# Placement of the weight ring and the activations in SBUF, in a float32r hybrid decoder block on one core

## Chip, cores, metric

One Trainium2 chip, one core. The time is the device time of one execution in microseconds (us), as a median over runs. Lower is better.

## What is computed

One decoder layer for 512 tokens of width 1024, in float32. The reference, cut to what matters:

```python
def hybrid_layer(x, ...):
    h = rms_norm(x, norm_mix_pre)
    u, v_sgu, q, k, v_att, gate_a, gate_b = split(h @ w_in)          # 1024 x 6656
    a = chunked_spatial_gating(gelu(u), gelu(v_sgu), ...)            # 128-token chunks, 8 groups
    att = sliding_window_sink_attention(rotary(q), rotary(k), v_att, sinks)
    merged = sigmoid(gate_a) * (a @ w_a) + sigmoid(gate_b) * (att @ w_b)
    x = x + rms_norm(merged @ w_o, norm_mix_post)
    hf = rms_norm(x, norm_ff_pre)
    ff = square(relu(hf @ w_ff_in)) @ w_ff_out                       # 1024 x 4096 x 1024
    return x + rms_norm(ff, norm_ff_post)
```

## The kernel before

Every large product is made of three float32r products. A weight and an activation are each split into a rounded part (hi) and the rest (lo), and TensorE adds hi x hi, hi x lo and lo x hi into the same PSUM bank. That is the helper `product`, whose three matmuls are lines 1125, 1126 and 1127:

```python
def product(o, a, b, first, last):
    (a_hi, a_lo), (b_hi, b_lo) = a, b
    nc.tensor.matmul(o, a_hi, b_hi, start=first, stop=False)
    nc.tensor.matmul(o, a_hi, b_lo, start=False, stop=False)
    return nc.tensor.matmul(o, a_lo, b_hi, start=False, stop=last)
```

The first operand `a` is stationary (loaded by an LDWEIGHTS of 128x128), the second, `b`, is moving (512 columns, in one place 256). In the rows of the trace the moving operand is named first: `acc<-actB_hi,w_hi` streams actB and holds w, `acc<-w_hi,ff_hi` streams w and holds ff.

Weights come through a ring of four slots (`SLOTS`) of one unit each, 128 x 1024 values. SyncE loads a unit into `w_raw` by DMA, ScalarE rounds it into `w_hi` (`round_unit`, line 563), VectorE writes the rest into `w_lo` (`lo_of`, line 799), and TensorE waits on `lo_made` before a unit. A slot is rounded again when TensorE is done with it (`pe_done`) and loaded again when `lo_made` has passed. 132 units go through the ring.

A unit is used in one of two ways. `columns_unit` holds the weights and streams the activations (8 products of 512 columns). `rows_step` holds the activations and streams the weights (2 products for each of 4 token tiles). Both are 24 matmuls a unit.

The stages in order, all written out by hand in the block `@block.tensor`, with the activations that they use and the count of matmuls of `product`:

- q, k, v projections: 12 units by rows, actB stationary, 288 matmuls
- gates and u (called side): 24 units by columns, actB moving, 576; the 16 steps of attention lie between them (`scores`, lines 1237 and 1238: kT moving, actA stationary; `turn_probs`, line 1247; `values`, lines 1263 and 1266: pT moving, v_pair stationary)
- v of the spatial gating: 8 units by rows, actB stationary, 192
- w_b: 8 units by columns, actA moving, 192, with the 64 matmuls of the spatial mixing (line 1312) between
- w_a: 8 units by columns, actB moving, 192
- w_o: 8 units by rows, actA stationary, 192
- feed-forward, in two halves of 2048: ff-in, 16 units by columns, actB moving (384 matmuls of 512 columns; in the first half the first four units are done as two halves of 256 columns, so 192 of 256 and 288 of 512), then ff-out, 16 units by rows, ff stationary, 384

SBUF addresses are given out in the order of the calls of `keep` and `group`, upward from 16.1 KiB. Tensors that live at different times share a place: a `with ExitStack()` gives the addresses back at its end, and `region_a` and `region_b` then claim the whole stretch. Each of w_raw, w_hi, w_lo, actB_hi, actB_lo, actA_hi and actA_lo takes 16 KiB of each partition.

```python
w_raw = keep("w_raw", [P, SLOTS, UNIT])
w_hi = keep("w_hi", [P, SLOTS, UNIT], F32R)
w_lo = keep("w_lo", [P, SLOTS, UNIT], F32R)
actB_hi = keep("actB_hi", [P, KT, S], F32R)
actB_lo = keep("actB_lo", [P, KT, S], F32R)
```

Of the kernel before, what the change touches and what calls it, by code (L numbers as in the profile page):

```python
# [35 lines left out]
F32 = mybir.dt.float32  # L36
F32R = mybir.dt.float32r
# [4 lines left out]
P = 128  # L42
D = 1024
S = 512
TT = S // P
KT = D // P
# [13 lines left out]
SLOTS = 4  # L60
UNIT = KT * P
# [156 lines left out]
def hybrid_block(nc, x, positions, w_in, ln_v_gain, ln_v_bias, w_spatial, b_spatial, sinks, w_a, w_b,  # L218
# [11 lines left out]
    with ExitStack() as ctx:  # L230
# [3 lines left out]
        def keep(name, shape, dt=F32):  # L234
            return ctx.enter_context(nc.sbuf_tensor(name, shape, dt))


        w_raw = keep("w_raw", [P, SLOTS, UNIT])
        w_hi = keep("w_hi", [P, SLOTS, UNIT], F32R)
        w_lo = keep("w_lo", [P, SLOTS, UNIT], F32R)  # L240


        actB_hi = keep("actB_hi", [P, KT, S], F32R)
        actB_lo = keep("actB_lo", [P, KT, S], F32R)
        ident = keep("ident", [P, P])
        mask = keep("mask", [P, 2 * P])
        pos_i = keep("pos_i", [P, TT], I32)
# [23 lines left out]
        denom2 = keep("denom2", [P, QPK])  # L271
        r_denom = keep("r_denom", [P, QPK])

        def group(stack, spec):
            return [stack.enter_context(nc.sbuf_tensor(n, s, d)) for n, s, d in spec]

        with ExitStack() as a:
            actA_hi, actA_lo = group(a, [("actA_hi", [P, KT, S], F32R), ("actA_lo", [P, KT, S], F32R)])  # L280
        with ExitStack() as a:
            ff_sum, g_ff_post, relu_b, sq_b, junk_ff = group(a, [
                ("ff_sum", [P, TT, D], F32), ("g_ff_post", [P, D], F32), ("relu_b", [P, 2, S], F32),
                ("sq_b", [P, 2, S], F32), ("junk_ff", [P, D], F32)])
        ctx.enter_context(nc.sbuf_tensor("region_a", [P, 2 * KT * S], F32))
        with ExitStack() as a:
            kT_hi, kT_lo, v_pair, o_part, o_sum, scores_sb, gates, probs, pT_hi, pT_lo, u_sb = group(a, [
                ("kT_hi", [P, NKV, S], F32R), ("kT_lo", [P, NKV, S], F32R),
                ("v_pair", [P, TT, NKV, 2 * HD], F32R), ("o_part", [P, 2, 2, P], F32),
                ("o_sum", [P, 2, 2, P], F32), ("scores_sb", [P, QPK, 2 * P], F32),  # L290
                ("gates", [P, 2 * KT, S], F32), ("probs", [P, QPK, 2 * P], F32),
                ("pT_hi", [P, 2, QPK * P], F32R), ("pT_lo", [P, 2, QPK * P], F32R),
                ("u_sb", [P, KT, S], F32)])
# [1117 lines left out]
```

## Time and profile before

| | us |
|---|---|
| median of 2 runs | 804.77 (804.72 to 804.82) |
| span of the profiled execution, first to last instruction | 802.8 |
| around that span, against the median | 2.0 |
| TensorE matmul busy | 790.7 (98%) |
| TensorE weight load busy | 659.3 (82%) |
| VectorE busy | 415.2 (52%) |
| ScalarE busy | 322.1 (40%) |
| GpSimd busy | 60.3 (8%) |

The page of the profile gives no time of the profiled execution beside its span; the 2.0 us are the median less the span. Matmuls are pipelined, so the busy time of one (some 390 ns for 512 columns) is longer than the distance from its start to the next one's. That distance is the length of a stretch divided by the matmuls that start in it.

### The profile page before, as it was taken

Reading aid. Unit: us, or ns where it says so; the run is one execution under the profiler, and the core shown is the slowest. Engines: PE = TensorE matmul, PEld = TensorE weight load, DVE = VectorE, ACT = ScalarE, POOL = GpSimd, SP = SyncE. Lnnn points to the kernel's source line nnn. Section 1 sums busy time; section 2 is a strip of 40 time slices with the busy share of each in tenths; the row PEclk is TensorE's granted clock in tenths of the full one; section 3 lists DMA queues with packets and bytes.
Section 4 is the critical chain, followed back from the end, with each engine's and each line's share of the span. In section 5 each row is a group of like instructions: output and inputs, shape, how many; then the busy total and the mean of one; then the engine's idle time right before and its main releaser. Section 6 shows DMA issues by size and latency. Waiting matters only on the chain.

```text
span 802.8 us, 10375 instructions
## 1 busy us (share of the span) xinstructions
PE 790.7 (98%) x3736; PEld 659.3 (82%) x3736; DVE 415.2 (52%) x730; ACT 322.1 (40%) x561; POOL 60.3 (8%) x110
## 2 busy tenths in 40 slices
PE   7999999999999999999999999999999999999996
PEld 6888888888887888888888988888888888888885
DVE  5624667777775329765536655432323354432334
ACT  4523656656666651323344444322212344322211
POOL 3000000122322003000002300000000000000001
PEclk9999999999999999999999999999999999999999
DMA  8332222222122532344331243332323333323202
GB/s 288 130 107 82 76 79 78 80 75 83 54 80 83 183 102 63 112 152 172 89 97 48 84 135 124 105 101 84 105 82 103 96 87 105 103 83 103 78 1 105
DMA packets 96215, 80.22 MB, mean 100 GB/s; under 512 B 3121, under 2 KB 77873, under 8 KB 96177
## 3 DMA queue, kind: packets, MB, share of 16 engines
q1 hardware_dynamic: 95504, 79.70, 32.0%
q8 instruction: 24, 0.39, 0.2%
q10 hardware_dynamic: 672, 0.01, 0.0%
q14 instruction: 15, 0.11, 0.0%
HBM read 77.60 MB, written 2.10 MB: 99 GB/s over the span
## 4 chain that ended last, share of the span: by engine, by line
PE 96%; DVE 2%; DMA 1%; ACT 1%; issue 0%; SPq 0%; DVEq 0%; POOLq 0%; POOL 0%; ACTq 0%
PE acc L1125 30%; PE acc L1127 30%; PE acc L1126 30%; PE aux L1312 1%; PE aux L1238 1%; DMA g_pre<-in_norm_mix_pre 1%; PE aux L1247 1%; PE aux L1237 1%; PE acc L1263 1%; PE acc L1266 1%; PE aux L1220 1%; PE aux L1167 1%; DVE x L818 0%; DVE actB_lo L809 0%; ACT probs L672 0%; DVE scores_sb L938 0%
## 5 line engine op out<-in xcount | busy, mean ns | idle before, releaser
L799 DVE TENSOR_TENSOR w_lo<-w_raw,w_hi 128x1024 fp32r<-128x1024 f32 x132 | 161.3, 1224 | 201.2 <-ACT w_hi L563 200.1
L563 ACT ACTIVATE w_hi<-w_raw 128x1024 fp32r<-128x1024 f32 x132 | 138.8, 1054 | 194.0 <-PE acc L1127 191.8
L1125 PE MATMUL acc<-actB_hi,w_hi 128*128 128x512 f32 (+1 forms) x544 | 207.1, 381 | 0.0
L1127 PE MATMUL acc<-actB_hi,w_lo 128*128 128x512 f32 (+1 forms) x544 | 205.3, 377 | 0.0
L1126 PE MATMUL acc<-actB_lo,w_hi 128*128 128x512 f32 (+1 forms) x544 | 204.9, 377 | 0.0
L1127 PEld LDWEIGHTS acc<-actB_hi,w_lo 128*128 128x128 f32 x544 | 102.4, 188 | 19.0
L1126 PEld LDWEIGHTS acc<-actB_lo,w_hi 128*128 128x128 f32 x544 | 102.5, 188 | 18.1
L1125 PEld LDWEIGHTS acc<-actB_hi,w_hi 128*128 128x128 f32 x544 | 102.4, 188 | 18.0
L1125 PE MATMUL acc<-w_hi,ff_hi 128*128 128x512 f32 x256 | 101.0, 395 | 0.0
L1127 PE MATMUL acc<-w_hi,ff_lo 128*128 128x512 f32 x256 | 101.0, 395 | 0.0
L1126 PE MATMUL acc<-w_lo,ff_hi 128*128 128x512 f32 x256 | 101.0, 395 | 0.0
L1125 PE MATMUL acc<-w_hi,actB_hi 128*128 128x512 f32 x160 | 62.7, 392 | 1.3 <-DVE actB_lo L809 1.2
L1073 DVE TENSOR_TENSOR sq_b<-relu_b 128x512 f32<-128x512 f32 x32 | 22.1, 692 | 80.2 <-ACT relu_b L761 79.9
L1126 PE MATMUL acc<-w_lo,actB_hi 128*128 128x512 f32 x160 | 62.3, 389 | 0.0
L1127 PE MATMUL acc<-w_hi,actB_lo 128*128 128x512 f32 x160 | 62.3, 389 | 0.0
L761 ACT ACTIVATE relu_b<-acc 128x512 f32<-128x512 f32 x32 | 19.2, 599 | 102.1 <-PE acc L1127 102.1
L1127 PEld LDWEIGHTS acc<-w_hi,ff_lo 128*128 128x128 f32 x256 | 48.2, 188 | 11.3
L1125 PEld LDWEIGHTS acc<-w_hi,ff_hi 128*128 128x128 f32 x256 | 48.2, 188 | 11.2
L1126 PEld LDWEIGHTS acc<-w_lo,ff_hi 128*128 128x128 f32 x256 | 48.2, 188 | 11.2
L672 ACT ACTIVATE probs<-scores_sb,neg_m 128x256 f32<-128x256 f32 (+1 forms) x64 | 30.1, 471 | 31.1 <-DVE sink_m L948 31.1
L1125 PEld LDWEIGHTS acc<-w_hi,actB_hi 128*128 128x128 f32 x160 | 30.0, 188 | 7.9 <-DVE actB_lo L809 1.8
L1127 PEld LDWEIGHTS acc<-w_hi,actB_lo 128*128 128x128 f32 x160 | 30.0, 188 | 6.2
(163 smaller groups left out, 897.7 us busy)
## 6 DMA issues: line engine op xcount, KB each, us to landing
w_raw<-in_w_in SPq DMA_DIRECT2D x44, 512.0 KB, 3.9
w_raw<-in_w_ff_in SPq DMA_DIRECT2D x32, 512.0 KB, 4.0
w_raw<-in_w_ff_out SPq DMA_DIRECT2D x32, 512.0 KB, 3.7
w_raw<-in_w_b SPq DMA_DIRECT2D x8, 512.0 KB, 3.6
w_raw<-in_w_a SPq DMA_DIRECT2D x8, 512.0 KB, 3.6
w_raw<-in_w_o SPq DMA_DIRECT2D x8, 512.0 KB, 3.8
x<-in_x SPq DMA_DIRECT2D x4, 512.0 KB, 7.4
x<-in_x SPq DMA_DIRECT2D x1, 2048.0 KB, 8.5
```

What stands on the lines that cost most here:

```text
L563: nc.scalar.activation(w_hi[:, j], w_raw[:, j], ACT.Copy).then_inc(hi_made, 1)
L672: nc.scalar.activation(probs[:, h, off:], scores_sb[:, h, off:], ACT.Exp, bias=neg_m[:, h:h + 1], accum_out=denom[:, h:h + 1])
L761: nc.scalar.activation(relu_b[:, j % 2], acc[:, j], ACT.Relu).then_inc(acc_to_act, 1)
L799: nc.vector.tensor_tensor(w_lo[:, j], w_raw[:, j], w_hi[:, j].bitcast(F32), ALU.subtract).then_inc(lo_made, 1)
L1073: nc.vector.tensor_tensor(sq_b[:, j % 2], relu_b[:, j % 2], relu_b[:, j % 2], ALU.mult).then_inc(sq_made, 1)
L1125: nc.tensor.matmul(o, a_hi, b_hi, start=first, stop=False)
L1126: nc.tensor.matmul(o, a_hi, b_lo, start=False, stop=False)
L1127: return nc.tensor.matmul(o, a_lo, b_hi, start=False, stop=last)
L1167: m = nc.tensor.transpose(aux[:, 2 * (t % 2) + k // 4, (k % 4) * P:(k % 4 + 1) * P], tile[:, t, k * P:(k + 1) * P], ident[:])
L1220: m = nc.tensor.transpose(aux[:, k % 4, t * P:(t + 1) * P], qk[:, t, 2 * k:2 * k + 2].rearrange("p h d -> p (h d)"), ident[:])
L1237: nc.tensor.matmul(o, q, kT_hi[keys], start=True, stop=False)
L1238: m = nc.tensor.matmul(o, q, kT_lo[keys], start=False, stop=True)
```

## The change

Only the addresses change. No instruction is added, removed, resized or moved in the order of any engine: each engine has as many instructions as before, in the same order, with the same waits. Every line of the body moves up by one number.

Places in SBUF, in KiB from the start of the partition:

| tensors | before | after |
|---|---|---|
| w_raw | 16.1 to 32.1 | 48.1 to 64.1 |
| w_hi, w_lo | 32.1 to 64.1 | 99.5 to 131.5 |
| actB_hi, actB_lo | 64.1 to 96.1 | 16.1 to 48.1 |
| region_a: actA_hi, actA_lo; later ff_sum, g_ff_post, relu_b, sq_b, junk_ff | 99.5 to 131.5 | 64.1 to 96.1 |
| constants and small tensors (ident, mask, ssq, ...) | 96.1 to 99.5 | the same |
| kT_hi, kT_lo (131.5 to 147.5), v_pair (147.5), o_sum, scores_sb, gates, probs, pT_hi, pT_lo (199.5 to 207.5), u_sb; v_sgu, w_mix; x1, ff_hi, ff_lo (147.5 to 211.5), mix | 131.5 and up | the same |

```diff
-        w_raw = keep("w_raw", [P, SLOTS, UNIT])
-        w_hi = keep("w_hi", [P, SLOTS, UNIT], F32R)
-        w_lo = keep("w_lo", [P, SLOTS, UNIT], F32R)
 
         actB_hi = keep("actB_hi", [P, KT, S], F32R)
         actB_lo = keep("actB_lo", [P, KT, S], F32R)
+        w_raw = keep("w_raw", [P, SLOTS, UNIT])
+
+        def group(stack, spec):
+            return [stack.enter_context(nc.sbuf_tensor(n, s, d)) for n, s, d in spec]
+
+        with ExitStack() as a:
+            actA_hi, actA_lo = group(a, [("actA_hi", [P, KT, S], F32R), ("actA_lo", [P, KT, S], F32R)])
+        with ExitStack() as a:
+            ff_sum, g_ff_post, relu_b, sq_b, junk_ff = group(a, [
+                ("ff_sum", [P, TT, D], F32), ("g_ff_post", [P, D], F32), ("relu_b", [P, 2, S], F32),
+                ("sq_b", [P, 2, S], F32), ("junk_ff", [P, D], F32)])
+        ctx.enter_context(nc.sbuf_tensor("region_a", [P, 2 * KT * S], F32))
         ident = keep("ident", [P, P])
...
         r_denom = keep("r_denom", [P, QPK])
 
-        def group(stack, spec):
-            return [stack.enter_context(nc.sbuf_tensor(n, s, d)) for n, s, d in spec]
...
-        with ExitStack() as a:
-            actA_hi, actA_lo = group(a, [("actA_hi", [P, KT, S], F32R), ("actA_lo", [P, KT, S], F32R)])
...
-        ctx.enter_context(nc.sbuf_tensor("region_a", [P, 2 * KT * S], F32))
+        w_hi = keep("w_hi", [P, SLOTS, UNIT], F32R)
+        w_lo = keep("w_lo", [P, SLOTS, UNIT], F32R)
         with ExitStack() as a:
             kT_hi, kT_lo, v_pair, o_part, o_sum, scores_sb, gates, probs, pT_hi, pT_lo, u_sb = group(a, [
```

## Rows read from the trace of the kernel before

**Rows 1.** Span and granted clock; the page's busy time of TensorE.
```profile
core 0: 802.8 us, clock 0.998
...
PE 790.7 (98%) x3736; PEld 659.3 (82%) x3736; DVE 415.2 (52%) x730; ACT 322.1 (40%) x561; POOL 60.3 (8%) x110
```

**Rows 2.** The chain that ended last, by engine.
```profile
PE 96%; DVE 2%; DMA 1%; ACT 1%; issue 0%; SPq 0%; DVEq 0%; POOLq 0%; POOL 0%; ACTq 0%
```

**Rows 3.** All waits of TensorE: us in total, times, longest.
```profile
PE acc L1176 <- POOL ident L479: 1.7, 1, 1.7
PE aux L1167 <- DVE x L818: 1.3, 1, 1.3
PE acc L1125 <- DVE actB_lo L809: 1.2, 1, 1.2
PE aux L1247 <- DVE probs L965: 1.2, 1, 1.2
```

**Rows 4.** TensorE by stretches: from:to, length, busy (instructions), clock, DMA share, GB/s.
```profile
37.87:81.39 43.52, 43.52 (x193) 1.00 0.38 115
...
298.97:350.82 51.85, 51.85 (x258) 1.00 0.28 83
350.82:394.39 43.57, 43.57 (x193) 1.00 0.46 157
394.39:416.70 22.31, 22.31 (x97) 1.00 0.38 110
...
465.50:530.81 65.31, 65.31 (x290) 1.00 0.37 112
530.81:620.05 89.24, 89.24 (x386) 1.00 0.31 96
620.05:707.10 87.05, 87.05 (x386) 1.00 0.32 95
707.10:796.10 89.00, 89.00 (x384) 1.00 0.22 73
```

**Rows 5.** The chain that ended last: one of the four pieces of spatial mixing within w_b; start, us.
```profile
321.52 1.78 PE aux L1312 x16
```

**Rows 6.** Groups by form: line, engine, out<-moving,stationary, count, busy, mean ns.
```profile
L1125 PE MATMUL acc<-actB_hi,w_hi 128*128 128x512 f32 x480 | 188.8, 393 | 0.0
...
L1125 PE MATMUL acc<-w_hi,actB_hi 128*128 128x512 f32 x160 | 62.7, 392 | 1.3 <-DVE actB_lo L809 1.2
...
L1125 PE MATMUL acc<-actB_hi,w_hi 128*128 128x256 f32 x64 | 18.3, 285 | 0.0
```

**Rows 7.** TensorE in order of time within one attention step: start, us.
```profile
166.15 0.39 PE L1125 MATMUL acc<-actB_hi,w_hi 128*128 128x512 f32 x1
166.38 0.39 PE L1126 MATMUL acc<-actB_lo,w_hi 128*128 128x512 f32 x1
166.60 0.40 PE L1127 MATMUL acc<-actB_hi,w_lo 128*128 128x512 f32 x1
166.84 0.39 PE L1263 MATMUL acc<-pT_hi,v_pair 128*128 128x512 f32 x1
167.07 0.39 PE L1266 MATMUL acc<-pT_lo,v_pair 128*128 128x512 f32 x1
167.29 0.39 PE L1263 MATMUL acc<-pT_hi,v_pair 128*128 128x512 f32 x1
167.52 0.39 PE L1266 MATMUL acc<-pT_lo,v_pair 128*128 128x512 f32 x1
167.75 0.28 PE L1237 MATMUL aux<-kT_hi,actA_hi 128*128 128x256 f32 x1
```

**Rows 8.** TensorE in the last steps of attention, columns as in rows 4.
```profile
240.00:254.00 14.00, 12.67 (x63) 1.00 0.26 75
```

**Rows 9.** Groups of ScalarE and VectorE that fill the ring.
```profile
L799 DVE TENSOR_TENSOR w_lo<-w_raw,w_hi 128x1024 fp32r<-128x1024 f32 x132 | 161.3, 1224 | 201.2 <-ACT w_hi L563 200.1
...
L563 ACT ACTIVATE w_hi<-w_raw 128x1024 fp32r<-128x1024 f32 x132 | 138.8, 1054 | 194.0 <-PE acc L1127 191.8
```

More of the change, by code:

```diff
@@ L272, in hybrid_block @@
         r_denom = keep("r_denom", [P, QPK])
-        def group(stack, spec):
-            return [stack.enter_context(nc.sbuf_tensor(n, s, d)) for n, s, d in spec]
-        with ExitStack() as a:
-            actA_hi, actA_lo = group(a, [("actA_hi", [P, KT, S], F32R), ("actA_lo", [P, KT, S], F32R)])
[L281 to L284, printed above, removed]
-        ctx.enter_context(nc.sbuf_tensor("region_a", [P, 2 * KT * S], F32))
+        w_hi = keep("w_hi", [P, SLOTS, UNIT], F32R)
+        w_lo = keep("w_lo", [P, SLOTS, UNIT], F32R)
         with ExitStack() as a:
```

## Prediction

> **What bounds the kernel now.** I read the span and the busy times first. TensorE is busy for 790.7 of 802.8 us [rows 1], and the chain that ended last is TensorE for 96% [rows 2]. Next the list of TensorE's waits: four rows, 5.4 us in all, three of them before or near the first products and one at the end of attention; none is for a weight, w_hi or w_lo [rows 3]. So loads, rounding and attention are hidden, and the time is the number of matmuls times the distance between their starts. A change that only moves addresses can act through that distance and hardly otherwise.
>
> Then I cut TensorE's time into stretches that hold nothing but products of 512 columns, and divided by the matmuls that the code issues there (the counts of the rows hold one or two more, which straddle an edge). The clock is 1.00 in each and there is no idle time, so a quotient is the distance itself [rows 4]:
>
> - second and third block of q, k, v (w moving, actB stationary): 43.52 / 192 = 226.7 ns
> - w_a (actB moving, w stationary): 43.57 / 192 = 226.9 ns
> - ff-in: 65.31 / 288 = 226.8 and 87.05 / 384 = 226.7 ns
> - first half of w_o (w moving, actA stationary): 22.31 / 96 = 232.4 ns
> - ff-out (w moving, ff stationary): 89.24 / 384 = 232.4 and 89.00 / 383 = 232.4 ns
> - w_b (actA moving, w stationary), less four pieces of 1.78 us of spatial mixing [rows 5]: (51.85 - 7.12) / 192 = 233.0 ns
>
> Shape, type, clock and helper are the same; what differs is where the operands lie. Where the distance is short, both operands lie under 96.1 KiB. Where it is long, w lies there and the other operand at 99.5 KiB or more. The step is 232.4 - 226.7 = 5.7 ns. The load on the other engines does not explain it: ff-in and ff-out take turns and the DMA share is 0.32 against 0.31, 0.37 against 0.22 [rows 4].
>
> Is it a high address that costs, or a pair on two sides? The attention steps tell. In `values` the moving pT (199.5 KiB) and the stationary v_pair (147.5 KiB) are both high. Starts at 167.07, 167.29, 167.52 and 167.75 are 0.22, 0.23 and 0.23 us apart, the short distance. The matmul ahead of them streams actB (low) while the weights loaded beside it are those of the next one, v_pair (high): from 166.60 to 166.84 is 0.24 us, the long one, and 166.15 to 166.38 to 166.60, low with low, is 0.23 and 0.22 [rows 7]. So what costs is a stream on one side of a boundary and a weight load on the other, in the one direction as in the other (actA is moving in w_b, stationary in w_o, and both have the long distance). The last pT_lo loads actA_hi at 99.5 KiB beside its stream from 203 KiB and has the short one, so actA is on the high side; the boundary lies between 96.1 and 99.5 KiB.
>
> **The change, part by part.** The edit moves the ring's two operands from the low to the high side (they stand where actA stood), actA from high to low, and leaves actB low (new place, same side) and ff, kT, v_pair, pT high. The rule above then gives:
>
> 1. Products with actB, 512 columns: 480 as moving and 160 as stationary operand [rows 6], three matmuls each, 1920. Low with low before, low with high after: 1920 x 5.7 ns = +10.94 us. TensorE has no idle time in these stretches, so all of it is on the path.
> 2. Products with ff: 32 units of 24, 768. High with low before, high with high after: 768 x -5.7 = -4.38 us.
> 3. Products with actA (w_b and w_o, 384 matmuls): the two operands change sides with each other, and the pair still crosses: 0.
> 4. The ff-in products of 256 columns, 64 x 3 = 192 [rows 6], go from low pairs to crossing ones. No row has 256 columns on a crossing pair. Ends: the whole step, 192 x 5.7 = +1.09, and nothing, if a shorter stream leaves the weight load as the limit and hides it. I see no reason for a gain. The nearest rows are the products of 512, so I take +1.09.
> 5. The scores, 16 steps of 8 = 128 matmuls by the code (kT moving, actA stationary, 96 of 256 columns and 32 of 128), go from high pairs to crossing ones. The same ends, 0 and +0.73; I take +0.73.
> 6. Turnovers between the kinds of matmul in an attention step: from pT to actA now crosses (16), from pT or probs to the ring's weights no longer does (16): 0.
> 7. The ring's feed. ScalarE's 1054 ns and VectorE's 1224 ns a unit now read w_raw low and write high. A unit lasts TensorE 24 x 0.227 = 5.4 us, the ring is four deep, and both engines idle before these instructions for 194 and 201 us in all [rows 9]. Were each 10% slower, that is 0.2 us against a lead of about three units: 0. If this cover were gone, 0.2 us a unit would be 132 x 0.2 = 26 us, and TensorE would show waits for w_lo.
> 8. What is given back: TensorE idles 14.00 - 12.67 = 1.33 us in the last attention steps, waiting for VectorE's chain [rows 8]. The products placed there as filler get longer: about 36 x 5.7 ns = 0.2 us of that idle time goes. -0.2 us.
> 9. The ends: up to 13.6 us and after 796.1 us no product of a changed pair decides. ff_sum moves to the low side for VectorE; three last instructions of 0.7 us, a few ns each at most: 0.
>
> Sum: 10.94 - 4.38 + 1.09 + 0.73 - 0.2 = +8.2 us. Against the profiled span: 802.8 + 8.2 = 811.0; the median of the runs stands 2.0 us over the span, so 804.77 + 8.2 = 812.9 us, slower by 1.0%. A measurement of this kernel can tell about 2% from no change, so this lies within that bound. Ends: with terms 4 and 5 at nothing 811.1; with a crossing step of 6.3 ns, as w_b has it, in place of 5.7, over the net 1920 - 768 + 320 matmuls, +0.9, so 813.8. A pair at new places may differ a little more, so the forecast's own range is 810.5 to 815.
>
> **What the Trainium skill says against it.** The rows show 226.7 ns with both operands low and 232.4 with one of each [rows 4]. "SBUF — State Buffer", section "Who interferes with whom", says that TensorE has one read port for the moving operand and another for the weight load, independent, that PE and ACT never wait on anyone, and that the only contention is on the pair which VectorE and GpSimd share. By that rule the place of an operand can't matter, terms 1 to 5 are all zero, and the time would stay at the present one. The rows differ from it: the same matmul costs 2.5% more in ff-out than in ff-in with no other engine in the way. I go by the rows.
>
> **Rivals.**
>
> A. The place does not matter, and the 5.7 ns belong to something else that comes with those stages, such as who else reads actB or ff. For it: stage and address change together in most rows. Against it: `values`, which reverts within one matmul. Time: 804.8 us.
>
> B. The ring's old low place is what costs toward high operands, and low actB with a high ring is not: then ff-out gains and nothing is lost. Time: 804.77 - 4.38 = 800.4 us, on the faster side, by ff-out stretches of 87.1 us with ff-in unchanged. It decides if the four ff-in and q, k, v stretches stay at 226.7 ns. For it: crossing was seen almost only with the ring as one partner. Against it: 166.60 to 166.84, where actB streams and v_pair is loaded, no part of the ring being read, has the long distance [rows 7].
>
> C. The cost grows with the distance of the two addresses. Now w at 99.5 and actB at 16.1 KiB are up to 115 KiB apart. Before, w_o (35 to 99 KiB apart) and ff-out (83 to 179 KiB apart) cost the same 232.4 ns [rows 4], so this is weak. If a larger step of 8 ns came with actB, it would be 1920 x 2.3 = 4.4 us on top: 817 us.
>
> **How the numbers follow.** Forecast 0.86, A 0.06, B 0.04, C or another larger cost 0.04. The forecast's own range holds about nine tenths of its case; I widen it at the low side to 809.5 and at the high side to 815.5, which leaves out A, B, C and the edges, some 2 in 10. All cases lie within 2% of 804.77 (788.7 to 820.9): within 2% 0.97, slower by more 0.02, faster by more 0.01.
>
> **What would show each step.** In the profile after, ff-in and q, k, v stretches at 232.4 ns (89.2 us for the second ff-in in place of 87.05), w_a 44.6 us, ff-out at 226.7 ns (87.1 us in place of 89.24), w_o unchanged at 22.3 us. The stretch with 256 columns, 24.7 us now, decides term 4: 25.8 or unchanged. The list of TensorE's waits should stay at four rows; a wait for w_lo would prove term 7 wrong. The forecast falls if ff-in keeps 226.7 ns (B), or if no stretch moves (A).

## Result and profile after

The changed kernel takes 812.22 us (811.28 and 813.17) against 804.77: a ratio of 1.0093, 95% interval 1.0077 to 1.0109. It is slower by 0.9%, clear of the noise but less than 2%. The profiled execution took 811.28 us with a span of 809.5. The forecast was 812.9 us, and 811.0 for the span. The execution of 813.17 us had a mean granted clock of 0.995 against 0.998 for the other; in later runs the kernel before took 806.5 to 807.0 us at 0.995 and 804.4 to 805.1 at 0.997 to 0.999.

First the page of the changed kernel, its busy times (against [rows 1]) and TensorE's waits (against [rows 3]):

```profile
PE 798.0 (99%) x3736; PEld 658.9 (81%) x3736; DVE 415.6 (51%) x730; ACT 322.3 (40%) x561; POOL 60.2 (7%) x110
```

```profile
PE acc L1175 <- POOL ident L478: 1.7, 1, 1.7
PE aux L1246 <- DVE probs L964: 1.2, 1, 1.2
PE acc L1124 <- DVE actB_lo L808: 1.2, 1, 1.2
PE aux L1166 <- DVE x L817: 0.7, 1, 0.7
```

There are still four waits and none for the ring. The other engines' busy times are the same to 0.4 us. The busy time of TensorE's matmuls is 7.3 us longer, the span 6.7.

TensorE by stretches in the changed kernel, from:to, length, busy (instructions), clock, DMA share, GB/s, to be laid beside [rows 4]; in order q, k, v (192 matmuls of `product`), w_b, w_a (192), the first half of w_o (96), ff-in of 256 columns, ff-in (288), ff-out (384), ff-in (384), ff-out:

```profile
38.15:82.95 44.80, 44.80 (x193) 1.00 0.37 111
304.33:356.25 51.92, 51.92 (x258) 1.00 0.28 82
356.25:401.05 44.80, 44.80 (x194) 1.00 0.42 153
401.05:423.45 22.40, 22.40 (x98) 1.00 0.39 111
447.55:472.10 24.55, 24.55 (x209) 1.00 0.39 110
472.10:539.30 67.20, 67.20 (x290) 1.00 0.36 111
539.30:626.36 87.06, 87.06 (x385) 1.00 0.31 97
626.36:715.96 89.60, 89.60 (x385) 1.00 0.30 94
715.96:802.79 86.83, 86.83 (x385) 1.00 0.22 73
```

The first line, 44.80 / 192 = 233.3 ns, had been 226.7. The second ff-in, 89.60 / 384 = 233.3, had been 226.7. ff-out, 87.06 / 384 = 226.7, had been 232.4. w_o and w_b stay long, at 22.40 / 96 and (51.92 - 7.12) / 192, both 233.3 ns. The stretch with the matmuls of 256 columns did not get longer. Before, it was

```profile
440.75:465.50 24.75, 24.75 (x210) 1.00 0.39 112
```

and now it is 24.55 us. So each stage of 512 columns went the way that the two-sides rule said. That the rule is the right one is a second question, and the experiments answered it otherwise.

### The profile page after: what moved, and what is told of

Read it like the earlier page. It is cut to its first block, busy times and chain, and to the rows that moved or that the text cites. A ratio compares the mean times of both kernels' runs of the same rounds, so it can differ in the third digit from the quotient of the medians.

```text
span 809.5 us, 10375 instructions
## 1 busy us (share of the span) xinstructions
PE 798.0 (99%) x3736; PEld 658.9 (81%) x3736; DVE 415.6 (51%) x730; ACT 322.3 (40%) x561; POOL 60.2 (7%) x110
## 4 chain that ended last, share of the span: by engine, by line
PE 96%; DVE 1%; DMA 1%; ACT 1%; issue 0%; SPq 0%; DVEq 0%; POOLq 0%; POOL 0%; ACTq 0%
PE acc L1124 30%; PE acc L1126 30%; PE acc L1125 30%; PE aux L1311 1%; PE aux L1237 1%; DMA g_pre<-in_norm_mix_pre 1%; PE aux L1246 1%; PE aux L1236 1%; PE acc L1265 1%; PE acc L1262 1%; PE aux L1219 1%; PE aux L1166 1%; DVE x L817 0%; DVE actB_lo L808 0%; ACT probs L671 0%; DVE scores_sb L937 0%
## 5 line engine op out<-in xcount | busy, mean ns | idle before, releaser
L1124 PE MATMUL acc<-actB_hi,w_hi 128*128 128x512 f32 (+1 forms) x544 | 209.4, 385 | 0.0
L1126 PE MATMUL acc<-actB_hi,w_lo 128*128 128x512 f32 (+1 forms) x544 | 207.6, 382 | 0.0
L1125 PE MATMUL acc<-actB_lo,w_hi 128*128 128x512 f32 (+1 forms) x544 | 207.5, 381 | 0.0
L1125 PEld LDWEIGHTS acc<-w_lo,ff_hi 128*128 128x128 f32 x256 | 48.1, 188 | 10.0
L1124 PEld LDWEIGHTS acc<-w_hi,ff_hi 128*128 128x128 f32 x256 | 48.1, 188 | 10.0
L1126 PEld LDWEIGHTS acc<-w_hi,ff_lo 128*128 128x128 f32 x256 | 48.1, 188 | 9.9
```

## Experiments

**The distances by place, with TensorE alone.** The stationary operand was held at ten places and the moving one at ten, 24 matmuls each:

```diff
+PLACES = (26, 48, 72, 92, 102, 120, 136, 160, 184, 216)   # KiB
+for s in PLACES:
+    for m in PLACES:
+        for n in range(24):
+            nc.tensor.matmul(acc[:, n % 4], at(s, P), at(m + 2, 512), start=True, stop=True)
```

> This kernel computes nothing of the layer: TensorE alone runs float32r matmuls on a constant, 24 in a row per pair of places, stationary and moving operand at ten places each (26 to 216 KiB), then the stationary one in steps of 0.5 KiB about 96 to 99.5 KiB, then 256 and 128 columns, then two alternations. Theory (a boundary between 96.1 and 99.5 KiB, the cost falls on a stream and a weight load on two sides): 512-column pairs at about 227 ns on one side, at 232 to 233 ns across, with no other engine at work; the steps show one jump. With own operands on one side and the next weights on the other, the alternation shows the long distance; with own operands across and the next weights on the stream's side, the short one. Rival A (place does not matter): one distance everywhere. Rival C (distance between addresses matters): it grows with the gap. For 256 columns the theory had 5.7 ns more across (120 to 126 ns); the changed kernel's stretch with 256 columns did not get longer, so a second form of it has no step there.

All hundred pairs together, TensorE by stretches of this probe:

```profile
64.19:602.75 538.56, 538.56 (x2378) 1.00 0.00 1
```

From the first matmul of the first pair to the first of the last pair there are 99 x 24 = 2376: 538.56 / 2376 = 226.7 ns. None of the pairs, across or not, was longer, nor was any of the steps about 96 KiB. At 256 columns all four pairings stood at 119.7 to 120.0 ns. The two alternations, where the theory had one long and one short, both ran at 226.7 ns, but for the first ten starts after the narrow matmuls ahead of them. Taken by itself this fits rival A and nothing of the two-sides theory, while the layer showed the step in every stage.

**Exchange actB and actA in the kernel before.**

```diff
 w_raw = keep(...); w_hi = keep(...); w_lo = keep(...)
-actB_hi = keep("actB_hi", [P, KT, S], F32R)
-actB_lo = keep("actB_lo", [P, KT, S], F32R)
+... actA and region_a here
 ident = keep("ident", [P, P])
...
 r_denom = keep("r_denom", [P, QPK])
-... actA and region_a here
+actB_hi = keep("actB_hi", [P, KT, S], F32R)
+actB_lo = keep("actB_lo", [P, KT, S], F32R)
```

> The kernel before with actB and region_a (actA) exchanged: actB at 99.5 to 131.5 KiB, actA at 64.1 to 96.1, the ring where it was. Theory: 1920 products with actB now cross (+5.7 to 6.6 ns each, +10.9 to +12.7 us), 384 with actA no longer do (-2.2 us), ff-out still crosses at 232.4 ns (0): +8.7 to +10.5 us, so 813.5 to 815.3 us. Rival B (the ring's place toward ff is what costs): ff-out stays as it was and nothing else changes but actA, 802.6 to 804.8 us. Rival C (a larger gap costs more): ff-in would be nearer 229 than 233 ns, as actB stands only 35 to 99 KiB from the ring.

Measured: 813.55 us, ratio 1.0105 (1.0089 to 1.0120). Stretches of w_b, the first ff-out, the second ff-in:

```profile
305.36:356.16 50.80, 50.80 (x258) 1.00 0.29 84
537.85:627.09 89.24, 89.24 (x385) 1.00 0.31 96
627.09:716.33 89.24, 89.24 (x385) 1.00 0.31 93
```

w_b is 1.05 us shorter, (50.80 - 7.12) / 192 = 227.5 ns; ff-in now costs 232.4 ns like ff-out. The ring was not touched, so the cost does not belong to the ring's place toward ff alone, which is what the expectation calls rival B. The prediction's own rival B is not tested here: a low ring with high operands costs under it too. The result had already put it out, with ff-in and q, k, v at 233.3 ns. Rival C had ff-in nearer 229 ns. The time is in the theory's range, at its low end.

**The ring high, actB where it was.** w_hi and w_lo change places with region_a.

```diff
 w_raw = keep("w_raw", [P, SLOTS, UNIT])
-w_hi = keep("w_hi", [P, SLOTS, UNIT], F32R)
-w_lo = keep("w_lo", [P, SLOTS, UNIT], F32R)
+... actA and region_a here
 actB_hi = keep(...); actB_lo = keep(...)
...
-... actA and region_a here
+w_hi = keep("w_hi", [P, SLOTS, UNIT], F32R)
+w_lo = keep("w_lo", [P, SLOTS, UNIT], F32R)
```

> The kernel before with the ring's w_hi and w_lo and region_a exchanged: the ring at 99.5 to 131.5 KiB as in the changed kernel, but actB still at 64.1 to 96.1 and actA at 32.1 to 64.1 KiB. Theory (only the side counts): the same as the changed kernel, +7.4 us, about 812.2 us, and ff-in at 233.3 ns. Rival C (the gap between the addresses counts; the crossing step came out at 6.6 ns instead of 5.7 because actB moved to 16.1 KiB): ff-in at 232.4 ns, 1920 x 0.9 = 1.7 us less, about 810.5 us.

Measured: 810.62 us, ratio 1.0068 (1.0053 to 1.0083). The q, k, v stretch, w_a and the second ff-in:

```profile
38.23:82.84 44.61, 44.61 (x194) 1.00 0.37 112
355.76:400.36 44.60, 44.60 (x193) 1.00 0.43 154
625.67:715.26 89.59, 89.59 (x385) 1.00 0.31 94
```

44.61 / 192 and 44.60 / 192 are 232.3 ns, and 89.59 / 384 = 233.3. w_a and ff-in both stream actB and hold w: the same tensors in the same roles, in one run, at both values. So 232.4 and 233.3 are two levels of one cost (two modes, below) and not a matter of the gap between the addresses. The total missed the theory's 812.2 by 1.6 us and looked like rival C's 810.5; the ff-in stretch, which C had at 232.4, rules C out.

**Everything that meets the ring on the high side.** A new layout: w_hi, w_lo, actB, actA or ff_hi, and gates or ff_lo from 96 to 224 KiB; all else below.

```diff
+w_raw = keep("w_raw", [P, SLOTS, UNIT])
+... small tensors; kT, v_pair, o_part, o_sum, scores_sb, probs, pT, u_sb and what shares their place
+keep("gap", [P, 120])
+w_hi = keep(...); w_lo = keep(...); actB_hi = keep(...); actB_lo = keep(...)
+... actA_hi, actA_lo, gates; later ff_hi, ff_lo
```

> A new layout: w_hi, w_lo, actB, then actA with gates and later ff_hi with ff_lo at 96 to 224 KiB; w_raw, constants, kT, v_pair, pT, x, mix, ff_sum and the rest under 95.5 KiB. All products of weights with activations have both operands on the high side. Theory: the 1152 crossing products of the kernel before (768 with ff, 384 with actA) come down from 232.4 to 226.7 ns: -6.6 us, 798.2 us; against the changed kernel -14 us. Scores, 256 columns, cross and cost nothing. Rival A: 804.8 us. Rival B (only a low ring toward high operands costs): 798.2 as well, so this run does not tell B apart, but shows whether the layout pays. If the high side is not one side (another boundary above 131.5 KiB), ff-out or w_b keeps 232 ns and the gain is 2 to 4 us.

Measured: 798.45 us, ratio 0.9922 (0.9908 to 0.9935), as forecast to 0.3 us. ff-out and ff-in:

```profile
529.07:616.11 87.04, 87.04 (x386) 1.00 0.32 98
616.11:703.15 87.04, 87.04 (x386) 1.00 0.32 96
```

Three layouts in a row came out within 1.6 us of where the two-sides theory put them. Had the place probe not been run, it would have passed for shown.

**What of the layer's sequence brings the cost back.** TensorE alone, but at the kernel's addresses, and with its sequence taken apart.

```diff
+W_HI, W_LO, FF_HI, FF_LO = 32896, 49280, 151040, 183808   # bytes
+for n, t, q in steps():                 # ff-out's order, hi and lo in turn
+    (ah, al), (bh, bl) = hold_ff(FF, n, q, t)
+    for i, (x, y) in enumerate(((ah, bh), (ah, bl), (al, bh))):
+        nc.tensor.matmul(acc[:, t], at(x, P), at(y, 512), ...)
...
+        m = nc.tensor.matmul(acc[:, i], at(FF_HI, P), at(W_HI, 512), start=True, stop=True)
```

> The place probe showed 226.7 ns across the two sides, with TensorE alone, fixed addresses, a new bank each time, and a constant as data, while the layer shows 232.4 across even where no other engine or transfer is at work. So the side alone does not cost; something in the sequence or the data does too. This kernel computes nothing of the layer. TensorE alone runs nine stretches of 96 matmuls of 512 columns at the addresses of the kernel before, in this order: ff-out's full sequence (hi and lo in turn, addresses that advance, six into a bank, accumulating); the same with actB in ff's place; ff-out's without accumulation; ff-out's with a new bank each time, no accumulation; ff-out's banks with fixed addresses; hi x hi alone with addresses that advance; hi and lo in turn at fixed addresses; the column form with actA moving; and fixed addresses, new bank, no accumulation. Then the same again with random numbers in place of the constant. Theory 1 (hi and lo in turn across the sides is what costs): 232.4 in stretches 1, 3, 4, 7, 8 and 226.7 in 2, 5, 6, 9, in both passes. Theory 2 (accumulation in PSUM together with the crossing): 232.4 in 1, 5, 6, 7, 8 and 226.7 in 2, 3, 4, 9. Theory 3 (the data: the products of numbers that toggle): 226.7 everywhere in the first pass, and 232.4 in the second in all but stretch 2. Theory 4 (the other engines or the transfers after all): 226.7 everywhere in both.

Stretches 2 (actB), 3 (ff, no accumulation) and 9 (ff_hi and w_hi at fixed addresses, new bank each time) of the first pass, 96 matmuls each:

```profile
92.82:114.63 21.81, 21.81 (x98) 1.00 0.00 1
114.63:136.94 22.31, 22.31 (x98) 1.00 0.00 1
248.48:270.79 22.31, 22.31 (x97) 1.00 0.00 1
```

21.81 / 96 = 227.2 ns (226.7 once its first eight are left out), 22.31 / 96 = 232.4 twice. Every stretch but the one with actB is at 232.3 to 233.3, in both passes. So all four theories fall: not the alternation, not accumulation, not the data, not the other engines. The last stretch is the place probe's own form, with 232.4 where the place probe had 226.7. All that is left between them is the addresses themselves. The place probe's are multiples of 1024 bytes. In the layer, tensors begin at 16512 bytes, 128 past a multiple of 256, and stay there up to the small tensors, which take 3456 bytes, 13.5 times 256; from there on all begin at a multiple of 256.

**The offset of one operand against the other, TensorE alone.**

```diff
+REPEAT = 48
+LOW_S, LOW_M, HIGH_M = 40 * 1024, 72 * 1024, 160 * 1024
...
+for s in range(0, 528, 16):
+    for n in range(REPEAT):
+        nc.tensor.matmul(acc[:, n % 4], at(LOW_S + s, P), at(LOW_M, 512), start=True, stop=True)
```

> In the structure probe the pairs across the sides cost 232 to 233 ns with TensorE alone, even at fixed addresses, and in the place probe the pairs across cost nothing. The two differ in this: all places of the place probe are multiples of 1024 bytes, while in the layer the low tensors start at 128 bytes past a multiple of 512 and the high ones at a multiple of 512, because the small tensors between them take 3456 bytes. This kernel computes nothing of the layer. TensorE alone, 48 matmuls of 512 columns a case: the stationary operand at 0, 16, 32 ... 512 bytes past 40 KiB with the moving one at 72 KiB; the moving one at 32, 64, 128, 256 bytes past, each with eight offsets of the stationary one; and four cases with the moving one at 160 KiB. Theory S (the two starts must agree in their lowest bits, the side is irrelevant): 226.7 ns where the offsets agree modulo some power of two up to 512, more elsewhere, and the same at 160 KiB as at 72 KiB; 232 to 233 ns for a difference of 128 bytes. Rival T (two sides, as predicted): 226.7 in all cases at 72 KiB, 232 or more in the four at 160 KiB.

48 matmuls a line. Stationary operand 0, 16, 32, 64, 128, 192, 256 and 384 bytes past its place, the moving one at a multiple of 1024; then both 128 past; then the moving one at 160 KiB with offsets (stationary, moving) of 0, 0, then 0, 128, then 128, 128:

```profile
71.62:82.50 10.88, 10.88 (x49) 1.00 0.01 2
82.50:93.39 10.89, 10.89 (x49) 1.00 0.00 0
93.39:104.58 11.19, 11.19 (x49) 1.00 0.01 1
115.78:126.97 11.19, 11.19 (x49) 1.00 0.00 0
160.53:171.73 11.20, 11.20 (x49) 1.00 0.01 1
205.16:216.16 11.00, 11.00 (x50) 1.00 0.00 0
249.45:260.33 10.88, 10.88 (x49) 1.00 0.01 2
338.36:349.56 11.20, 11.20 (x49) 1.00 0.01 1
660.91:671.78 10.87, 10.87 (x49) 1.00 0.01 2
793.77:804.66 10.89, 10.89 (x50) 1.00 0.00 0
804.66:815.85 11.19, 11.19 (x50) 1.00 0.01 1
827.04:837.92 10.88, 10.88 (x49) 1.00 0.00 0
```

10.88 / 48 = 226.7 ns where the two offsets agree modulo 256 bytes (or differ by 16, which theory S did not have), 11.19 and 11.20 / 48 = 233.1 to 233.3 for 32, 64 and 128 bytes of difference, 229.2 for 192; the second 256 bytes repeat the first. At 160 KiB it is the same, so the side does not matter and only the difference does. Theory S holds, with 256 for the power of two; T falls.

**128 unused bytes in each of the two kernels.** The same line in both:

```diff
         r_denom = keep("r_denom", [P, QPK])
+        keep("offset", [P, 32])
```

> The kernel before with one unused tensor of 128 bytes behind the small tensors: every high tensor moves up by 128 bytes and then starts, like the low ones, 128 bytes past a multiple of 512. No tensor changes its side. Theory S: the 1152 products with ff and actA come down from 232.4 to 226.7 ns: -6.6 us, 798.2 us. Rival T (two sides): 804.8 us.

> The changed kernel with the same 128 bytes behind the small tensors. Theory S: all products at 226.7 ns, 798.2 us, 14 us less than the changed kernel, and the same as the kernel before with the 128 bytes. Rival T (two sides): 812.2 us.

Measured, on one chip: 798.17 us, ratio to the kernel before 0.9918 (0.9905 to 0.9930), and 798.33 us, ratio 0.9916 (0.9903 to 0.9928). The kernel before with 128 bytes, w_b, first ff-out, second ff-in:

```profile
299.26:349.98 50.72, 50.72 (x258) 1.00 0.29 85
528.96:616.00 87.04, 87.04 (x386) 1.00 0.33 98
616.00:703.04 87.04, 87.04 (x386) 1.00 0.32 96
```

The changed kernel with 128 bytes, ff-out and ff-in:

```profile
529.61:616.65 87.04, 87.04 (x386) 1.00 0.31 98
616.65:703.69 87.04, 87.04 (x386) 1.00 0.32 95
```

With the offsets equal, it makes no difference where the ring stands: 798.2 and 798.3. The whole effect of the change is in which operands' offsets differ. Either beats both kernels of this case.

**The converse: a mismatch without crossing.** The 128 bytes stand before actB.

```diff
         w_lo = keep("w_lo", [P, SLOTS, UNIT], F32R)
+        keep("offset", [P, 32])
         actB_hi = keep("actB_hi", [P, KT, S], F32R)
```

> The kernel before with the 128 bytes between the ring and actB. Ring and actB stay on the low side, ff and actA on the high one; but actB now starts at a multiple of 256 bytes where the ring starts 128 past one, and all that lies above (actA, ff, kT, pT, v_pair) is 128 past one, like the ring. Theory S: the 1920 products with actB go from 226.7 to 232.3 or 233.3 ns, the 1152 with ff and actA come down to 226.7: the same as the changed kernel, or a little under it as w_b and w_o gain too: -6.6 + 10.8 to 12.7, so 809 to 811 us. Rival T (two sides): no operand changes its side, 804.8 us.

Measured: 811.13 us, ratio 1.0067 (1.0042 to 1.0091), with every tensor on its old side: just above theory S's 809 to 811 us, where T had 804.8. w_b, first ff-out and second ff-in:

```profile
306.60:357.36 50.76, 50.76 (x257) 1.00 0.29 84
539.07:626.13 87.06, 87.06 (x385) 1.00 0.32 97
626.13:715.72 89.59, 89.59 (x385) 1.00 0.31 93
```

These are the 227.3, 226.7 and 233.3 ns of theory S. That the total comes so near to the changed kernel's is chance. The stretches of w_b and w_o are 2.3 us shorter than there, but at 23.7 us the profiled execution was already 2.4 us behind the changed kernel's. TensorE was busy for 5.95 of its first 10 us (7.52 in the changed kernel), and then its granted clock stood at the lower level, 1.2 GHz, for a while:

```profile
14.00:18.00 4.00, 3.90 (x9) 0.50 0.72 265
```

In the changed kernel's trace the clock is 1.00 in that stretch. The one execution of four with a mean clock of 0.998 took 809.2 us, the others, at 0.994, 811.05 to 811.76.

**How wide a matmul has to be.**

```diff
+for cols in (512, 448, 384, 320, 256, 192, 128):
+    for s in (0, 64, 128):
+        for n in range(REPEAT):
+            mm = nc.tensor.matmul(acc[:, n % 4, 0:cols], at(LOW_S + s, P), at(LOW_M, cols), start=True, stop=True)
```

> This kernel computes nothing of the layer. TensorE alone, 48 matmuls a case at 512, 448, 384, 320, 256, 192 and 128 columns, the stationary operand 0, 64 and 128 bytes past the moving one's place in its 256. Theory: at 512 columns 226.7, 233.3 and 232 to 233.4 ns as in the offset probe. At 256 columns the layer shows no cost (119.6 ns with the 128-byte difference, 120.6 without), so the cost ends somewhere between. If it is a fixed toll per matmul, 320 to 448 columns show 6 ns too and 256 also would, against the layer; if the toll grows with the columns streamed beside the weight load, 384 shows about half of it; if the toll belongs to 512 alone, 448 shows none.

Differences of 0 and 128 bytes at 512, 448, 384 and 256 columns:

```profile
71.56:82.44 10.88, 10.88 (x50) 1.00 0.01 2
93.63:104.79 11.16, 11.16 (x49) 1.00 0.01 1
104.79:114.52 9.73, 9.73 (x49) 1.00 0.00 0
124.23:134.01 9.78, 9.78 (x49) 1.00 0.01 2
134.01:142.36 8.35, 8.35 (x49) 1.00 0.00 0
150.84:159.29 8.45, 8.45 (x50) 1.00 0.01 2
180.40:186.14 5.74, 5.74 (x51) 1.00 0.00 0
191.80:197.49 5.69, 5.69 (x50) 1.00 0.00 0
```

Per matmul the 128 bytes cost (11.16 - 10.88) / 48 = 5.8 ns at 512 columns, 1.0 at 448, 2.1 at 384, nothing at 320 (7.03 and 7.04 us for the 48), and gain 1.0 at 256. A fixed toll is ruled out, and so are the other two forms of the expectation: the cost neither grows evenly with the columns, as 448 has less than 384, nor belongs to 512 alone. Its course between 256 and 512 columns is measured but not explained. Without a difference, the columns at 2.4 GHz (granted clock 1.00) and 13.3 ns more make up the distance at 512 columns (226.7 ns) and, to 0.4 ns, at 256 (119.6); at 448 it is 2.7 ns longer than that (202.7).

## Why the prediction was right, and where its reasons were not

**What bounds the kernel.** Right: four waits as before, and the span follows the distance between matmuls alone.

**The rule.** The prediction put it thus: "what costs is a stream on one side of a boundary and a weight load on the other". Wrong as a mechanism. There is no boundary. The small tensors between 96.1 and 99.5 KiB take an odd number of 128-byte steps, 27, so the tensors under them and over them differ by 128 bytes modulo 256. In every row of the trace before the two readings say the same, as they do in the changed kernel and in three of my layouts. So it was luck that the wrong rule gave the right sign and nearly the right size: had the change brought 128 bytes more, the same reasoning would have said what it said, and 798.3 us was measured. The place probe (226.7 ns across) contradicted it, the offset probe and the three versions with 128 bytes settled it.

One step of its evidence stands under the new reading: a stream and the weight load beside it, the next matmul's, are enough for the cost. At the turn from actB's products to pT's each matmul's own two operands have equal offsets, but the stream of one and the load of the other do not. The starts across that turn lie 233 ns apart in the kernel before, as the median of the 16 steps, and 227 in the same kernel with 128 bytes, where all offsets agree.

**Term 1**, +10.94 us. The stretches give +1.28 (q, k, v), +1.23 (w_a), +1.89 and +2.55 (ff-in), at 6.4 to 6.7 ns a matmul and not 5.7: these stages went to the mode of 233.3 ns, while the 5.7 came from w_o and ff-out, which stood in that of 232.4. The prediction had a row of the other mode, w_b with 233.0 ns, and used it only as an end of the range. Against that, the stretch of attention with gates and u between grew by only 2.18 us. Before, then after:

```profile
108.48:254.55 146.07, 144.74 (x731) 1.00 0.26 76
```

```profile
110.50:258.75 148.25, 146.98 (x732) 1.00 0.25 75
```

It holds 480 products of term 1, which were to cost 2.7 us, and the 128 scores of term 5. The products of actB in it, without the first of each step, went from 227.7 to 232.5 ns, a step of 4.8. That they stood at 227.7 and not at 226.7 before has nothing to do with offsets: with all offsets equal, in the kernel before with 128 bytes, it is 227.9. All stretches with actB and attention together come to +11.2 us, where terms 1, 5 and 8 had 11.5.

**Term 2**, -4.38 us: 87.06 - 89.24 and 86.83 - 89.00, -4.35. Right.

**Term 3**, 0: w_b +0.07 us and the first half of w_o +0.09. Right; w_o went to the other mode, w_b was in it.

**Term 4**, +1.09 us: 24.55 - 24.75 = -0.2. Mis-sized, and the sign is wrong: I gave the 256 columns the whole step of 512 and saw no reason for a gain. At 256 columns a difference of 128 bytes gains 1 ns, as the width probe has it.

**Term 5**, +0.73 us: nothing. From one score of 256 columns to the next it was 119.0 ns before, the mean of 84 distances, and 118.2 after. The same error as in term 4.

**Terms 7 and 9**, 0: no wait for w_lo, the same busy times, and 6.7 us from TensorE's last start to the end of the span both times. Right. **Term 6**, 0: the turn from pT to actA went from 227 to 231 ns, 14 times, which is under 0.1 us. Right. **Term 8**, -0.2 us: TensorE's idle time in the attention stretch, 1.33 us before and 148.25 - 146.98 = 1.27 after. Smaller, and nearly nothing.

Terms 4 and 5 were 2.0 us too high. With them right, the span would have been forecast at 809.0; it came out at 809.5. Against the profiled execution, 811.28 us, the forecast of 812.9 was 1.6 us too high. The 812.22 lies nearer only because the second execution took 813.17, at the lower clock.

**The Trainium skill.** The prediction weighed the rule of "SBUF — State Buffer", "Who interferes with whom", that PE never waits on anyone and its two read ports are independent. The runs show 226.7 ns at equal offsets at any of a hundred pairs of places, which agrees with it: the place is indeed free. They show up to 234 ns at unequal offsets (at a difference of 96 bytes) with no other engine at work, which it doesn't tell. No other engine is waited for, but the starts of TensorE's own two operands in SBUF are not without effect on each other.

**The rivals.** A was nearer the truth than I gave it credit for: the place does not matter, and something else came with it. But its time, 804.8, was wrong, since that something is also an address. B fell to the result itself by the sign that the prediction gave, as ff-in and q, k, v left 226.7 ns. C fell to the layout with the ring high, and to the place probe, where pairs 192 KiB apart had 226.7 ns.

## What to carry to other kernels

Where TensorE is the bound with float32r matmuls of 512 columns, start every tensor that it reads at the same offset modulo 256 bytes, and pad the small tensors between them to a multiple of 256; here one unused tensor of 128 bytes gave 0.8%. Divide a stretch by its count of matmuls, stage by stage, and compare: the 226.7 and 232.4 ns of ff-in and ff-out are hard to see in the mean busy times of line 1125, 393 and 395 ns. And when a theory of addresses fits all stages, write down the other property that the same addresses share, and break the two apart before believing either.

## What the hardware showed that I had not expected

- The distance between two matmuls of 512 columns depends on the difference of the two operands' starts modulo 256 bytes: 226.7 ns at 0, about 227 at 16 to either side, 233.1 at 32, 229.2 at 192, with TensorE alone and at any place tried.
- A mismatch of 128 bytes has two modes, 232.4 and 233.3 ns, at the same addresses: 11.20 us for 48 matmuls in the offset probe and 11.16 in the width probe, and both in one run of the layer. What sets the mode was not found.
- The effect shrinks fast under 512 columns: of 128 bytes 1.0 ns is left at 448, 2.1 at 384, nothing at 320, and at 256 the mismatch gains 1.0.
- Why 256 bytes, and what in the two reads collides, if anything does, stays open.
- The transposes with ident, 128 columns, pay nothing: those of mix follow each other at 109.0 ns in the kernel before, where mix and ident differ by 128 bytes, and in the same kernel with 128 bytes, where they agree.
